# Five small re-orderings in a kernel of two transformer blocks: first load, values' buffer, last expert, groups, last signal

## The reference

```python
# first block
h  = rms_norm(x); z = h @ w_in                   # a pool part, and 8 heads of attention (4 pairs)
x  = x + concat(pool(z), attention(q, k, v)) @ w_out
for e in range(16):                              # 16 experts, each takes 32 of the 256 rows
    xe = rows chosen by the router
    x += scatter((silu(xe @ w_gate[e]) * (xe @ w_up[e])) @ w_down[e])
x  = x + sigmoid(rms_norm(x) @ w_ple_gate) * rms_norm(p @ w_ple_proj)
# second block
h  = rmsnorm(x); z = h @ w_in_2
y_nsa = compressed, selected and window attention, 4 groups of 4 heads
y_ml  = mlstm(silu(causal_conv(q, k)), v, gates)          # 4 heads
y_mem = attention over a memory of 256 rows                # 4 heads
x  = x + rmsnorm((sum of the three, gated and projected) @ w_out_2)
h  = rmsnorm(x); gate, up = split(h @ w_ffn_in)            # width 2816
x  = x + rmsnorm((silu(gate) * up) @ w_ffn_down)
```

## Time and profile before

| | |
|---|---|
| median of 3 runs | 1687.64 us |
| the three runs | 1682.1, 1687.64, 1687.9 us |
| the profiled execution's own time | 1681.77 us |
| its span | 1680.0 us |
| mean granted TensorE clock | 0.914 of full |
| busy: TensorE, VectorE, ScalarE, GpSimd | 1356.1, 512.5, 188.5, 39.4 us |
| HBM read | 515.53 MB, 307 GB/s over the span |

### The profile page before, as it was taken

One profiled execution on the slowest core, in us unless ns is written; L12 is line 12 of the kernel. 1 busy time (PEld: TensorE's weight loads), 2 busy tenths in 40 slices (PEclk: granted clock), 3 DMA queues, 4 the chain that ended last, 5 costly groups with the idle time before them and its releaser, 6 DMA issues. The chain is left out here.

```text
span 1680.0 us, 21172 instructions
## 1 busy us (share of the span) xinstructions
PE 1356.1 (81%) x8808; PEld 779.6 (46%) x8808; DVE 512.5 (31%) x1055; ACT 188.5 (11%) x496; POOL 39.4 (2%) x104
## 2 busy tenths in 40 slices
PE   8998666676657666865676588999999999999997
PEld 5543121121113111311121133787778999599953
DVE  2433011011101101110100110445545664477875
ACT  2330010000000000000000000214343100100000
POOL 1100000000000000000000000000000000000000
PEclk9999798788889878977887899999999999999999
DMA  9668999999999999999999999513341442444332
GB/s 400 247 244 363 429 434 427 430 434 427 433 427 435 428 431 432 431 430 432 430 431 430 433 426 430 219 66 116 113 165 69 185 165 86 200 151 151 125 145 81
DMA packets 30332, 517.98 MB, mean 308 GB/s; under 512 B 3392, under 2 KB 4416, under 8 KB 6848
## 3 DMA queue, kind: packets, MB, share of 16 engines
q1 hardware_dynamic: 28352, 514.01, 73.1%
q10 hardware_dynamic: 1920, 3.10, 0.5%
HBM read 515.53 MB, written 1.05 MB: 307 GB/s over the span
## 5 line engine op out<-in xcount | busy, mean ns | idle before, releaser
L983 PE MATMUL ps<-ring,scr 128*32 128x512 f32 (+2 forms) x3130 | 480.9, 742 | 250.7 <-DMA ring<-in_experts 246.0
L983 PEld LDWEIGHTS ps<-ring,scr 128*32 128x32 f32 (+1 forms) x3130 | 122.9, 134 | 582.9 <-issue 309.1
L983 PE MATMUL ps<-turned_T,ring 128*128 128x128 f32 (+1 forms) x1760 | 244.5, 299 | 1.8 <-DVE scr L2058 1.0
L983 PEld LDWEIGHTS ps<-turned_T,ring 128*128 128x128 f32 x1760 | 227.5, 192 | 15.5 <-issue 5.5
L983 PE MATMUL ps<-scr 128*128 128x128 f32 (+12 forms) x908 | 167.6, 381 | 18.2 <-DVE scr L1917 12.2
L983 PEld LDWEIGHTS ps<-scr 128*128 128x128 f32 (+4 forms) x908 | 95.3, 176 | 85.3 <-issue 47.2
L983 PE MATMUL ps<-ring,turned_T 128*128 128x128 f32 (+3 forms) x512 | 128.7, 409 | 1.1 <-DMA ring<-in_w_in 1.1
L983 PEld LDWEIGHTS ps<-ring,turned_T 128*128 128x128 f32 x512 | 82.2, 191 | 44.8 <-issue 31.7
L1920 DVE TENSOR_TENSOR x<-x,ps 128x512 f32<-128x512 f32 x60 | 41.2, 687 | 199.9 <-PE ps L983 199.9
L1910 DVE SCALAR_TENSOR_TENSOR scr<-scr,ps 128x512 f32<-128x512 f32 x16 | 11.0, 688 | 295.1 <-PE ps L983 295.1
L1908 DVE SCALAR_TENSOR_TENSOR scr<-scr,ps 128x512 f32<-128x512 f32 x16 | 11.0, 687 | 228.1 <-ACT scr L771 228.1
(11 more groups left out here) (307 smaller groups left out, 1023.3 us busy)
## 6 DMA issues: line engine op xcount, KB each, us to landing
ring<-in_experts SPq DMA_DIRECT2D x70, 4096.0 KB, 22.9
ring<-in_experts SPq DMA_DIRECT2D x48, 2048.0 KB, 21.7
ring<-in_w_ffn_in SPq DMA_DIRECT2D x11, 2048.0 KB, 7.8
ring<-in_w_merge SPq DMA_DIRECT2D x10, 2048.0 KB, 7.8
ring<-in_w_ffn_down SPq DMA_DIRECT2D x11, 1024.0 KB, 4.8
ring<-in_w_out SPq DMA_DIRECT2D x4, 2048.0 KB, 26.0
ring<-in_w_ml SPq DMA_DIRECT2D x4, 2048.0 KB, 7.7
ring<-in_w_nsa SPq DMA_DIRECT2D x4, 2048.0 KB, 7.7
```

The source lines that it names most:

```text
L983: return pe.matmul(o, l, rr, start=start, stop=stop)
```

## The change

It has six parts, all in the order or the place of work, and no product, copy or byte is added or taken away:

- SP issues the first megabyte of `w_in` in two halves, the first with a semaphore of its own, `in_w_head`; TensorE waits for the first at k = 0, for the other at k = 2.
- The values of pair j go to a buffer `vA` with two places (in `xn`, which is unused at that time) instead of `zA`; `projected_v` moves ahead of the copy of the attention result, and ScalarE's loop over pairs is written out.
- In the last expert strips 8 and 9 are loaded one by one, and TensorE runs y, folded, gates for each i in turn.
- In the groups the two `yc` products move ahead of the wait for `qm` and of the memory scores.
- Three of `conv(1)`'s eight products (in the last group half of `first_gates(1)`) move between `turned(n4, 2)` and `turned(n4, 3)`, and with them the wait for `ynsa_done`.
- Product q = 3 of the last step signals too, and VectorE starts the sums of banks 2 and 3 on it.

```diff
--- before.py
+++ after.py
@@ -297,6 +297,7 @@
         A = Area()
         poolm = A(NT * 4 * T, "p (t g s) -> p t g s", t=NT, g=4)
         mx = A(NT * D, "p (t d) -> p t d", t=NT)
+        vA = xn.rearrange("p t d -> p (t d)")[:, 0:4 * P].rearrange("p (j k n) -> p j k n", j=2, k=NT)
         zA = A(NT * 512, "p (t n) -> p t n", t=NT)
         sqA = A(NT * T, "p (t n) -> p t n", t=NT)
         qkn = A(NT * T, "p (t n) -> p t n", t=NT)
@@ -467,6 +468,7 @@
             sem(n) for n in ("mg_ps", "mp_ps", "mg_th", "mg_free", "out2_ps", "y_sq", "x4_done"))
         ff_ps, ff_th, ff_h, ffo_ps = sem("ff_ps"), sem("ff_th"), sem("ff_h"), sem("ffo_ps")
         fold_ps, fold_sb = sem("fold_ps"), sem("fold_sb")
+        in_w_head = sem("in_w_head")
         ff_sum, mg_sum, mg_sb = sem("ff_sum"), sem("mg_sum"), sem("mg_sb")
         tfull = [full[n] for n in TAIL]
         landed, merge_landed = {}, {}
@@ -487,7 +489,8 @@
 
             for t in range(NT):
                 sp.dma_start(x[:, t, :], a["x"][0][t * P:(t + 1) * P, :]).then_inc((in_x, in_x1)[t], 16)
-            first, rest = slice(0, SLOT // 2), slice(SLOT // 2, SLOT)
+            head, first, rest = slice(0, SLOT // 4), slice(SLOT // 4, SLOT // 2), slice(SLOT // 2, SLOT)
+            sp.dma_start(slot[0][:, head], a["w_in"][0, :, head]).then_inc(in_w_head, 16)
             sp.dma_start(slot[0][:, first], a["w_in"][0, :, first]).then_inc(in_w_first, 16)
             r.load(0, (slot[0][:, rest], a["w_in"][0, :, rest]))
             sp.dma_start(btab.rearrange("p h r c -> p (h r c)"), a["bias"]).then_inc(in_tables, 16)
@@ -555,14 +558,14 @@
             slots = around(ROT)
             sp.wait_ge(mkv_ps, 4)
             sp.dma_start(slot[9][:, 0:SLOT], a["w_ple_gate"][0]).then_inc(full[9], 16)
-            for n in range(0, 10, 2):
+            for n in range(0, 8, 2):
                 s = slots[n]
                 r.load_two(s, ring[:, s * SLOT:(s + 2) * SLOT], packed["experts"][bass.ds((LAST * 6 + n // 2) * P, P), :])
                 if n == 2:
                     sp.wait_ge(e_sq, 2)
                     sp.dma_start(later[:, 0:SLOT // 2], a["w_ple_gate"][1, :, 0:SLOT // 2]).then_inc(full[6], 16)
                     sp.dma_start(turned_T[:, KC * T:], a["w_ple_gate"][1, :, SLOT // 2:SLOT]).then_inc(full[7], 16)
-            for n in (10, 11):
+            for n in (8, 9, 10, 11):
                 r.load(slots[n], strip_of(slots[n], LAST, n))
 
 
@@ -703,9 +706,9 @@
                     act.activation(zA[:, t, 0:384], bank[t][:, 0:384], ACT.Copy, scale=rst[:, t:t + 1]).then_inc(zA_sb, 1)
 
             def projected_v(j):
-                act.activation(zA[:, 0, 384:512], bank[0][:, 384:512], ACT.Copy, scale=rst[:, 0:1]).then_inc(vA_sb, 1)
+                act.activation(vA[:, j % 2, 0, :], bank[0][:, 384:512], ACT.Copy, scale=rst[:, 0:1]).then_inc(vA_sb, 1)
                 act.wait_ge(zA_ps, j * 3 + 3)
-                act.activation(zA[:, 1, 384:512], bank[5][:, 0:P], ACT.Copy, scale=rst[:, 1:2]).then_inc(vA_sb, 1)
+                act.activation(vA[:, j % 2, 1, :], bank[5][:, 0:P], ACT.Copy, scale=rst[:, 1:2]).then_inc(vA_sb, 1)
 
             def pooled(j):
                 act.wait_ge(poolA_ps, j + 1)
@@ -727,20 +730,16 @@
                        .then_inc(ptA_sb, 1)
                 if more:
                     pooled(j + 1)
+                    projected_v(j + 1)
                 act.wait_ge(oA_ps, j * 2 + 2)
-                act.nop(nofuse=True)
-                act.activation(yT[:, bass.ds(j + 4, 1), :].rearrange("p a t -> p (a t)"), bank[6][:, 0:T], ACT.Copy)\
-                   .then_inc(yA_attn, 1)
-                if more:
-                    projected_v(j + 1)
+                act.activation(yT[:, j + 4, :], bank[6][:, 0:T], ACT.Copy).then_inc(yA_attn, 1)
 
             act.wait_ge(rs_done, 2)
             projected(0)
             projected_v(0)
             pooled(0)
-            with act.Fori(0, PAIRS - 1) as j:
-                pair(j, True)
-            pair(PAIRS - 1, False)
+            for j in range(PAIRS):
+                pair(j, j < PAIRS - 1)
 
 
             act.wait_ge(in_mem, 32)
@@ -1022,6 +1021,8 @@
                 for t in range(NT):
                     for k in range(KC):
                         if (j, t) == (0, 0) and k == 0:
+                            pe.wait_ge(in_w_head, 16)
+                        if (j, t) == (0, 0) and k == 2:
                             pe.wait_ge(in_w_first, 16)
                         if j is FIRST and k % 4 == 0:
                             pe.wait_ge(hT_done, 1 + 2 * t + k // 4)
@@ -1079,7 +1080,7 @@
                 pe.wait_ge(ptA_sb, j * 2 + 2)
                 for k in range(NT):
                     for h in range(2):
-                        ins = mm(bank[6][64 * h:64 * h + 64, 0:T], zA[:, k, 384 + 64 * h:448 + 64 * h],
+                        ins = mm(bank[6][64 * h:64 * h + 64, 0:T], vA[:, j % 2, k, 64 * h:64 * h + 64],
                                  PTA[:, h, k, :], k == 0, k == NT - 1)
                         if k == NT - 1:
                             ins.then_inc(oA_ps, 1)
@@ -1299,7 +1300,7 @@
             def last_y(i):
 
                 s = slots[8 + i]
-                arrived(s, 8 + i, False)
+                arrived(s, 8 + i, True)
                 tall = slot[s].rearrange("p (k n) -> p k n", k=16)
                 for k in range(16):
                     row, c = divmod(k, 4)
@@ -1355,13 +1356,7 @@
                     gate_product(1, 1, range(KC))
             h_turned(LAST, slots)
             pe.wait_ge(ht_sb, LAST + 1)
-            last_y(0)
-            last_y(1)
-            last_folded(0)
-            last_folded(1)
-            last_gates(0)
-            last_gates(1)
-            for i in (2, 3):
+            for i in range(4):
                 last_y(i)
                 last_folded(i)
                 ins = last_gates(i)
@@ -1423,9 +1418,11 @@
                         ins.then_inc(tfree[5], 1)
             ins.then_inc(cmp_ps, 1)
 
-            def conv(m):
-
-                return product(bank[7 - m][:, T:2 * T], lambda k: tstrip[0][:, k, m * P:(m + 1) * P])
+            def conv(m, ks=range(KC)):
+
+                for k in ks:
+                    ins = mm(bank[7 - m][:, T:2 * T], tstrip[0][:, k, m * P:(m + 1) * P], hT[:, k, :], k == 0, k == KC - 1)
+                return ins
 
             r.arrived(0, 1)
             for m in range(2):
@@ -1487,10 +1484,10 @@
                 r.arrived(MERGE_SLOTS[n], 1)
                 merge_landed[n] = r.incs[MERGE_SLOTS[n]]
 
-            def first_gates(j):
+            def first_gates(j, fs=range(2)):
 
                 w = tstrip[MERGE_SLOTS[GATES0]]
-                for f in range(2):
+                for f in fs:
                     for k in range(4):
                         ins = mm(bank[7 - j][:, T + f * P:T + (f + 1) * P], w[:, 4 * j + k, f * P:(f + 1) * P],
                                  hT[:, 4 * j + k, 0:P], k == 0, k == 3)
@@ -1526,16 +1523,15 @@
                     if k == 0:
                         ins.then_inc(tfree[0], 1)
                 ins.then_inc(proj_ps, 1)
+                pe.wait_ge(c_qk, g + 1)
+                mm(bank[6][:, 0:T], yc[:, 1, 0:P], yc[:, 0, :])
+                mm(bank[6][:, T:T + P], yc[:, 1, P:T], yc[:, 0, P:T])
                 pe.wait_ge(proj_sb, g * 7 + 6)
                 for t in range(NT):
                     ins = mm(bank[4][:, t * T:(t + 1) * T], qm[:, t * P:(t + 1) * P], kTm[:, bass.ds(g * T, T)])
                     if t == 0:
                         ins.then_inc(tfree[1], 1)
                 ins.then_inc(xs_ps, 1)
-
-                pe.wait_ge(c_qk, g + 1)
-                mm(bank[6][:, 0:T], yc[:, 1, 0:P], yc[:, 0, :])
-                mm(bank[6][:, T:T + P], yc[:, 1, P:T], yc[:, 0, P:T])
 
                 pe.wait_ge(staged, g * 7 + 7)
                 pe.nop(nofuse=True)
@@ -1588,18 +1584,21 @@
                     ins = mm(bank[0][:, 0:T], vmg[:, k, :], PTm[:, k, :], k == 0, k == NT - 1)
                 ins.then_inc(xo_ps, 1)
                 turned(n4, 2)
+                pe.wait_ge(ynsa_done, g * 2 + 1)
+                pe.nop(nofuse=True)
+                if more:
+                    conv(1, range(3))
+                else:
+                    first_gates(1, range(1))
                 turned(n4, 3)
                 pe.wait_ge(ym_sb, g + 1)
                 for t in range(NT):
                     ins = pe.transpose(bank[2][:, t * P:(t + 1) * P], y1[:, t, :], ident)
                 ins.then_inc(ym_ps, 1)
                 if more:
-                    pe.wait_ge(ynsa_done, g * 2 + 1)
-                    pe.nop(nofuse=True)
-                    conv(1).then_inc(proj_ps, 1)
+                    conv(1, range(3, KC)).then_inc(proj_ps, 1)
                 else:
-                    pe.wait_ge(ynsa_done, g * 2 + 1)
-                    first_gates(1).then_inc(mg_ps, 1)
+                    first_gates(1, range(1, 2)).then_inc(mg_ps, 1)
```

(7 more changed lines are left out.)

## The result

| | before | after |
|---|---|---|
| median | 1687.68 us (1682.1 to 1687.9, 4 runs) | 1666.43 us (1666.35 to 1666.76, 4 runs) |
| ratio | | 0.9888, interval 0.9865 to 0.991 |
| the profiled execution's own time | 1681.77 us | 1666.4 us |
| its span | 1680.0 us | 1664.6 us |
| mean granted TensorE clock | 0.914 | 0.917 |

The changed kernel is faster, by 21.2 us between the medians and by 15.4 us between the two profiled executions. The 21.2 are partly chance: executions of either kernel now and then take 5 to 7 us more, and three of the four of before did, none of the four of after. In a longer series on one chip, with 28 executions of before and 6 of after, the medians were 1681.37 and 1666.62 us. Between executions at the lower level the change is worth 15 us.

What follows compares the result with a forecast made beforehand. The expert-weight stream sets the pace, with TensorE busy behind it; an earlier TensorE moves the stream one for one. Terms 0.9 + 2.0 + 4.4 + 6.2 + 0.85 = 14.3 us, forecast 1673.3 from the median, range 1664 to 1682.

Steps and rivals of the forecast that it cites:

- Rival B: Start of the expert-weight stream: no earlier, so time saved ahead of it is hidden; 11.4 us gained, 1676.2; chance 0.04.
- Part 1: Kernel start: the first megabyte loaded in two halves lets products start earlier; 0.9 us taken, from 0.6 to 1.1.
- rival C: Added DMAs at the start and last expert: each costs a serial 2 us; 12.2 us gained, 1675.4; chance 0.03.
- Part 2: Pairs 1 to 3: the values' own buffer removes the scores' wait for ScalarE's copies, 2.0 us; written-out loop taken at 0.
- Part 3: Last expert: strips 8 and 9 loaded singly, y(0) bound by the hidden state at full clock; y(3) 4.4 us earlier.
- Rival A: Last expert: the clock stays low or strip 8 lands late; 2 to 3.4 us less, 1675.3 to 1676.7; chance 0.10.
- the order one by one costs nothing: Last expert: y, folded, gates in turn cost nothing; two strips took 11.05 us together, 9.6 in series.
- Part 4: Four groups: moved products fill gaps ahead of the memory scores and the fourth turning; 6.2 us, at least 4.5.
- Rival E: Groups: the filled gaps return one wait later; up to 5 of 6.2 us lost, 1678.5; chance 0.08.
- Part 5: Kernel end: an earlier signal from the fourth product cuts VectorE's idle time; 0.85 us, bounds 0.4 to 0.86.
- The step from the profile to the median: Whole-kernel time: the forecast was made from the median, 5.9 us above the profiled run, giving 1673.3 instead of 1667.5.
- Rival D: Expert-weight stream of 917 us: runs slower, each percent costing 9.2 us, nothing left from 1.6% on; chance 0.08.

Runs made afterwards that it cites:

- the head alone: Only the first megabyte of `w_in` loaded in two halves, against the kernel before: 1680.65 us against 1681.48, ratio 0.9994.

## Why the prediction was right

**The bound.** Right. That the stream starts earlier by what TensorE gains ahead of it was read from idle DMA engines in the earlier trace rows; 3.14 us came off the stream's start, and 3.10 were still there in the last expert. Rival B falls.

**Part 1.** 0.9 predicted, 0.95 between the two profiles, 0.77 in the profile of the head alone, 0.8 in the times. The pieces land 1.2 and about 2.4 us apart, by their size alone; rival C falls. Of the Trainium skill, DMA: Bandwidth & Descriptors, section "Anatomy of one DMA", gives each DMA on gpsimd's path a fixed part of about 2 us, mostly its completion. It doesn't say that queued DMAs pay it one after the other; that was rival C's reading. The trace doesn't contradict the page for one DMA, but of DMAs queued behind each other on SP's queue no such part is seen: with one more of them the first product started at 8.55 us in the head experiment, where the turns of x start at 6.71 as in before (6.73), instead of at 9.81.

**Part 2.** 2.0 predicted, 2.19 found, and the written-out loop, taken at 0 with bounds from nothing to a loss, was a gain that the bounds left out: 0.17 us a pair. It didn't show in the sum, since it is part of the wait that goes.

**Part 3.** 4.4 predicted, 4.39 between the two profiles, 4.1 by the experiment. That the first two agree so closely is in part luck: the forecast was worked out from the profile that it is compared with, and against four other profiles of the same stage it would be 3.6 to 3.8. The mechanism was as said: y(0) bound by the hidden state, the clock not falling, y(3) ahead by the chain of about 4.8 us per strip (4.80 to 4.89 in after). Rival A falls. The step "the order one by one costs nothing" holds with single transfers: about 0.3 us in its favour.

**Part 4.** 6.2 predicted, 7.04 in the traces, 6.9 by the experiment. The mechanism was right and the term too small. The gap of 0.57 us gave 0.65 in start-to-start time, that of 0.99 gave 1.18. The idle time in brackets is counted from the end of the product before, and neighbouring products overlap: in the earlier trace rows 16 passes start at 1147.91 and last 3.72, so they end at 1151.63, while the next product in that timeline starts at 1151.56. The rows of after show 0.17 us for a turning (1148.39 + 0.82, the next at 1149.04). A gap therefore costs its bracket and the overlap of 0.07 to 0.19 us that it breaks. The pairs show the same (0.66 and 0.73). Rival E falls: no wait came back at the values. (Its price is 0.2 too high by its own terms: 5 of 6.2 lost makes 1678.3, not 1678.5.)

**Part 5.** 0.85 predicted, 0.86 in both traces.

**The sum** was 14.3 us, and 15.4 came between the profiles: 0.8 of the 1.1 missing is part 4, 0.2 part 2. From the profiled time it gave 1667.5 us, and the profiled run of after took 1666.4. Against the 14.75 us of the longer series it is 0.4 short, as part 4's miss and what part 3 took from one slow profile have opposite signs.

**The step from the profile to the median** is the one that failed. I added the 5.9 us by which the median stood above the profiled run and forecast 1673.3. Of the executions of before in the experiments 17 of 78 were at the higher level, so the two of three times that the forecast had, and the three of four in the first comparison, were a poor guide, and the next median fell into the lower level, as most do. The range had been drawn to hold both clusters and did, and the measured time lies 1.1 us from what the sum gives from the profiled run, but 6.9 from the forecast. Rival D, a slower stream, falls with the slices above; the 5.8 us that spoke for it are not the stream's in the one high execution that has a profile, but TensorE's clock in one stage (5.6 us).

## What to carry to other kernels

Ask of each wait what is late next, and of time ahead of a stream whether the stream starts earlier for it: with both read from the trace, five small terms added up to within 8% of the whole. Look at the stage in more than one profile before its size is taken: one stage differed by 0.8 us between executions of the same code. Price a TensorE gap by start-to-start times, not by the idle time alone. When a few runs of before fall into two clusters, forecast from the cluster that the profile belongs to and say the other beside it, rather than carry the chance offset of a small median along.

## What the runs showed of the hardware

- **Half clock under full load.** TensorE ran at a granted clock of 0.50 for 13.5 us while busy all the time, in one execution and not in others with the same products before it; it cost 5.6 us. Of the Trainium skill, TensorE: Matmul & The Clock Gate, section "HAM oscillation", tells of waits on DMA that throw the engine back to half rate. The last expert agrees: 3.7 us of waiting, then 3.46 us for a y product that takes 1.93, and with 0.69 us of waiting (in other experiments 1.07 and 1.81 us) the clock stayed. The compression stage has no such wait: 0.73 us ahead of it, in the high execution and in the others.
- **Changing between kinds of product.** Passes of 64 rows by 75 columns and of 128 rows by 256 columns, alternating in blocks of 16 and 2, cost 0.17 us at each change (2.7 us for 16).
- **A loop on ScalarE** with a copy whose place depends on the loop's register (and an empty instruction ahead of it) started that copy 0.17 us later after its release than the written-out one.
- **Queued transfers on one queue** landed apart by their bytes alone: 0.5 MB after 1.2 us, 1 MB after 2.4 (before; 2.3 in after), 2 MB after 4.9 (strips 10 and 11 of the last expert in before).
